# Two transformer blocks on one core: stage borders without drains, small products moved between slabs, and the state-space decays computed from one 128-row product

## What is computed

```python
def mla_branch(u, cos, sin, q_norm_g, w_uq, kv_norm_g, w_ukv, q_gain, k_gain):
    c_q, c_kv, k_rope = jnp.split(u, [MLA_Q_RANK, MLA_Q_RANK + MLA_KV_RANK], axis=-1)
    q = (rms_norm(c_q, q_norm_g) @ w_uq).reshape(Bsz, S, MLA_HEADS, MLA_QK_DIM)
    kv = (rms_norm(c_kv, kv_norm_g) @ w_ukv).reshape(Bsz, S, MLA_HEADS, MLA_NOPE + MLA_V)
...
def ssd_scan(x, dt, A, Bm, Cm):
    a_cum = jnp.cumsum(dtc * A.astype(jnp.float32).reshape(G, Hg), axis=2)
    seg = a_cum[:, :, :, None] - a_cum[:, :, None, :]
    decay = jnp.where(causal, jnp.exp(jnp.where(causal, seg, 0.0)), 0.0)
    cb = jnp.einsum('bcign,bcjgn->bcijg', Cc, Bc)
    y_diag = jnp.einsum('bcijg,bcijgh,bcjghp->bcighp', cb, decay, xdt)
...
def gated_linear_attention(q, k, v, r, a_lr, w_a2, b_a, norm_g):
    log_a = jax.nn.log_sigmoid(jnp.einsum('bsr,rk->bsk', a_lr.astype(f32), w_a2.astype(f32))
                               + b_a.astype(f32)) / GLA_TAU
```

## Time and profile before

| | us |
|---|---|
| median of 3 runs | 2051.41 (2048.81 to 2052.89) |
| profiled execution | 2049.72 |
| its span, first to last instruction | 2048.0 |
| TensorE busy | 2010.6 |
| VectorE busy | 1146.9 |
| ScalarE busy | 805.7 |
| GpSimd busy | 111.7 |

### The profile page before, as it was taken

How to read it: one execution, slowest core, us unless ns; L and a number is a source line. 1 busy time by engine, 2 the same in 40 slices (tenths; PEclk the granted TensorE clock), 3 DMA queues, 4 the chain that set the end, 5 groups by cost and what they waited for, 6 DMA issues and landing times.

```text
span 2048.0 us, 23834 instructions
## 1 busy us (share of the span) xinstructions
PE 2010.6 (98%) x9734; PEld 1649.8 (81%) x9734; DVE 1146.9 (56%) x1680; ACT 805.7 (39%) x1146; POOL 111.7 (5%) x120
## 2 busy tenths in 40 slices
PE   7999999999999999999999999999999999999998
PEld 6887788777888888888888687888888888888886
DVE  5757657577444666357468877743435444234346
ACT  5647543344422434134242634542323433123245
POOL 0004400221000000000010300000000000000000
PEclk9999999999999999999999999999999999999999
DMA  4320022212332333333332123223222232332222
GB/s 133 103 83 22 17 87 84 91 59 70 130 103 82 94 92 103 99 87 93 112 125 92 53 75 101 83 83 103 85 100 103 83 103 83 103 114 87 98 103 82
DMA packets 164443, 184.46 MB, mean 90 GB/s; under 512 B 6759, under 2 KB 125798, under 8 KB 164334
## 3 DMA queue, kind: packets, MB, share of 16 engines
q1 hardware_dynamic: 161006, 175.03, 26.8%
q10 hardware_dynamic: 2624, 5.78, 0.8%
q0 software_dynamic: 704, 2.13, 0.3%
HBM read 180.81 MB, written 2.12 MB: 89 GB/s over the span
## 4 chain that ended last, share of the span: by engine, by line
PE 94%; DVE 3%; issue 2%; ACT 1%; POOL 0%; DMA 0%; DVEq 0%; SPq 0%; POOLq 0%; ACTq 0%
PE ps L448 29%; PE ps L450 29%; PE ps L449 29%; PE ps L591 1%; PE ps L605 1%; PE ps L578 1%; PE ps L639 1%; DMA W<-in_w_in_dram 0%; PE ps L826 0%; ACT HH L1372 0%; DVE arena L2078 0%; PE ps L562 0%; DVE HL L1998 0%; DVE WL L1881 0%; PE ps L747 0%
## 5 line engine op out<-in xcount | busy, mean ns | idle before, releaser
L448 PE MATMUL ps<-HH,WH 128*128 128x512 f32 (+1 forms) x1464 | 561.6, 384 | 6.9 <-DVE HL L1998 2.9
L1881 DVE TENSOR_TENSOR WL<-W,WH 128x2048 fp32r<-128x2048 f32 (+2 forms) x162 | 366.5, 2263 | 355.7 <-ACT WH L1322 355.3
L450 PE MATMUL ps<-HH,WL 128*128 128x512 f32 (+1 forms) x1464 | 557.5, 381 | 0.0
L449 PE MATMUL ps<-HL,WH 128*128 128x512 f32 (+1 forms) x1464 | 557.4, 381 | 0.0
L1322 ACT ACTIVATE WH<-W 128x2048 fp32r<-128x2048 f32 (+2 forms) x163 | 307.2, 1886 | 290.3 <-DMA W<-in_w_ff_dram 116.2
L448 PEld LDWEIGHTS ps<-HH,WH 128*128 128x128 f32 x1464 | 276.2, 189 | 64.5 <-issue 6.6
L450 PEld LDWEIGHTS ps<-HH,WL 128*128 128x128 f32 x1464 | 275.9, 188 | 52.6
L449 PEld LDWEIGHTS ps<-HL,WH 128*128 128x128 f32 x1464 | 276.3, 189 | 51.8 <-issue 0.2
L448 PE MATMUL ps<-WH,arena_r 128*128 128x512 f32 (+1 forms) x616 | 239.6, 389 | 1.6 <-issue 1.6
L450 PE MATMUL ps<-WH,arena_r 128*128 128x512 f32 (+1 forms) x616 | 239.1, 388 | 0.0
L449 PE MATMUL ps<-WL,arena_r 128*128 128x512 f32 (+1 forms) x616 | 239.0, 388 | 0.0
(11 more groups left out here) (372 smaller groups left out, 2278.6 us busy)
## 6 DMA issues: line engine op xcount, KB each, us to landing
W<-in_w_in_dram SPq DMA_DIRECT2D x50, 1024.0 KB, 5.1
W<-in_w_ff_dram SPq DMA_DIRECT2D x32, 1024.0 KB, 5.2
W<-in_ffn_w_up_dram SPq DMA_DIRECT2D x44, 512.0 KB, 4.7
W<-in_w_gate_dram SPq DMA_DIRECT2D x16, 1024.0 KB, 5.0
W<-in_ffn_w_down_dram SPq DMA_DIRECT2D x10, 1024.0 KB, 5.0
W<-in_w_out_dram SPq DMA_DIRECT2D x8, 1024.0 KB, 5.1
W<-in_w_branch_dram SPq DMA_DIRECT2D x8, 1024.0 KB, 5.0
W<-in_w_br_ssm_dram SPq DMA_DIRECT2D x4, 1024.0 KB, 5.0
```

Of the source, the lines that this page charges most:

```text
L448: pe.matmul(out_, st[0], mv[0], start=first, stop=False)
L449: pe.matmul(out_, st[0], mv[1], start=False, stop=False)
L450: return pe.matmul(out_, st[1], mv[0], start=False, stop=last)
L1881: dve.tensor_tensor(WL[:, j % RING, 0:n], W[:, j % RING, 0:n], plain(WH[:, j % RING, 0:n]), ALU.subtract).then_inc(slab_lo, 1)
```

## The change

It does four things. (1) TensorE's drain at the end of each stage is gone; the other engines wait in `boundary` for a count of TensorE's results. (2) In mla the four parameter transposes stand between the two tiles of the second slab, and `kr` and `cstat` between the two halves of `uq`, with the splits of ScalarE and VectorE counted anew. (3) In the scan the row of sums is one product of 128 rows: its stationary operand U has ones in the rows 0 to 47 and the negated sums of the token tile in 64 to 111, and the moving one, written by GpSimd on all 128 rows, the diagonals and one-hot rows that pick the head. So PSUM holds a(i) - a(j) for four heads. ScalarE takes Relu of its negative into M, then Exp of the negative of that; `diff` is gone, and `mix` works in place in a ring of three. The diagonals have one buffer. The order of VectorE's and ScalarE's steps is changed, and the split of the next but one slab stands before the gates. (4) In gla the two `la` products stand behind the first token tile of `gv`.

```diff
--- before.py
+++ after.py
@@ -655,41 +660,44 @@
+                def parameters():
+                    pe.wait_ge(params_in, 16 * (len(place) - len(first_params)))
+                    for j in range(1, NPAR):
+                        b = bank(("par", j))
+                        pe.transpose(b[:, 0:P], rows[:, j, :], ident[:, :]).then_inc(pe_done, 1)
                 for i in range(2):
                     w = slab(KT, 256, win(256 * i, 256 * i + 256))
                     if i == 0:
                         gemm_f_by_halves("c", w, 2, first_parameters)
                     else:
-                        gemm_f("c", w, KT, 0, 2, hn, 2 * i)
+                        gemm_f("c", w, KT, 0, 2, hn, 2 * i, parameters)
                     slab_read()
-                    if i == 0:
-                        pe.wait_ge(params_in, 16 * (len(place) - len(first_params)))
-                        for j in range(1, NPAR):
-                            b = bank(("par", j))
-                            pe.transpose(b[:, 0:P], rows[:, j, :], ident[:, :]).then_inc(pe_done, 1)
...
-                taken(pe, ("c", 5))
-                b = bank("kr")
...
-                b = bank("cstat")
...
+                taken(pe, ("c", 2))
                 for half in range(2):
                     w = slab(3, 384, A["mla_w_uq"][0].rearrange("(k p) n -> p k n", p=P)[:, :, half * 384:half * 384 + 384])
                     gemm_t("uq", w, 3, 0, 384, lambda k, t: [c[:, k, t * P:(t + 1) * P] for c in cg], half)
                     slab_read()
+                    if half == 0:
+                        taken(pe, ("c", 5))
+                        b = bank("kr")
+                        for t in range(NT):
+                            tr = pe.transpose(b[:, t * ROPE:(t + 1) * ROPE], at(1024, S)[0:ROPE, t * P:(t + 1) * P],
+                                              ident[0:ROPE, 0:ROPE])
...
+                        b = bank("cstat")
+                        taken(pe, ("c", 4))
+                        pe.wait_ge(square_sums, 2)
...
@@ -793,11 +802,9 @@
                     def arow(q):
-                        i = 4 * t + q
-                        rs = slice(64 * (i % 2), 64 * (i % 2) + 48)
                         b = bank(("ai", t, q))
-                        pe.wait_ge(diagonals_ready, i + 1)
-                        pe.matmul(b[:, :], bc(unit[rs, 0:1], [48, P]), split_at(19456, S)[rs, :],
+                        pe.wait_ge(diagonals_ready, 4 * t + q + 1)
+                        pe.matmul(b[:, :], split_at(25088, NT, P)[:, t, :], split_at(19456, S),
                                   start=True, stop=True).then_inc(pe_done, 1)
@@ -823,7 +830,7 @@
                         pe.wait_ge(mix_ready, 4 * t + q + 1)
                         for j in range(4):
                             h = 4 * q + j
-                            mm = pe.matmul(b[:, (h % 8) * HD:(h % 8 + 1) * HD], M[:, q % 2, j, :],
+                            mm = pe.matmul(b[:, (h % 8) * HD:(h % 8 + 1) * HD], M[:, (4 * t + q) % 3, j, :],
                                            xdt[:, h * HD:(h + 1) * HD], start=True, stop=True)
+                def decays(t):
+                    if t == 0:
+                        pe.wait_ge(decay_in, 16)
+                        taken(pe, ("gasm", 0))
+                        for c in range(2):
+                            b = bank(("la", c))
+                            pe.matmul(b[:, :], wa2[0:16, c * P:(c + 1) * P], alr[0:16, :],
+                                      start=True, stop=True).then_inc(pe_done, 1)
+                gemm_t_long("gv", full, 1536, hnt, between=decays)
@@ -1131,7 +1141,7 @@
             for s in stages:
                 program[s]()
                 stage_slabs.append(len(slabs) - 1)
-                pe.drain().then_inc(tensor_end, 1)
+                stage_done.append(len(DONE))
         def boundary(eng, own, k):
 
             eng.drain().then_inc(own, 1)
-            for end in (tensor_end, scalar_end, vector_end, gpsimd_end):
+            eng.wait_ge(pe_done, stage_done[k])
+            for end in (scalar_end, vector_end, gpsimd_end):
                 if end is not own:
                     eng.wait_ge(end, k + 1)
                 def diagonal(i):
                     t, q = divmod(i, 4)
-                    rs = slice(64 * (i % 2), 64 * (i % 2) + 48)
-                    if i >= 2:
-                        use(pool, ("ai", (i - 2) // 4, (i - 2) % 4))
-                    pool.tensor_tensor(split_at(19456, 4, P)[rs], bc(plain(mask_r[rs, t * P:(t + 1) * P]).unsqueeze(1), [48, 4, P]),
-                                       bc(pick[rs, 4 * q:4 * q + 4].unsqueeze(2), [48, 4, P]), ALU.mult)\
+                    if i >= 1:
+                        use(pool, ("ai", (i - 1) // 4, (i - 1) % 4))
+                    pool.tensor_tensor(split_at(19456, 4, P), bc(plain(mask_r[:, t * P:(t + 1) * P]).unsqueeze(1), [P, 4, P]),
+                                       bc(pick[:, 4 * q:4 * q + 4].unsqueeze(2), [P, 4, P]), ALU.mult)\
...
                 diagonal(0)
-                diagonal(1)
...
+                    diagonal(4 * t + 1)
...
-                    for i in range(4 * t + 2, min(4 * t + 6, 4 * NT)):
+                    for i in range(4 * t + 2, min(4 * t + 5, 4 * NT)):
                         diagonal(i)
...
-                split(slab_of["kr"] + 2)
+                split(slab_of["c", 5] + 2)
-                tmp, xt = at(24576, 2, 512), at(12288, NT, DM)
+                M, xt = at(23552, 3, 512), at(12288, NT, DM)
 
                 def decay(i):
+                    b = use(act, ("ai", i // 4, i % 4))
+                    if i >= 3:
+                        t, q = divmod(i - 3, 4)
+                        use(act, ("yd", t, q // 2)) if q % 2 == 1 else act.wait_ge(yc_ready, 2 * t + q // 2 + 1)
+                    freed(act.activation(M[:, i % 3, :], b[:, :], ACT.Relu, scale=-1.0), ("ai", i // 4, i % 4))
                     taken(act, ("ai", i // 4, i % 4))
-                    act.activation(tmp[:, i % 2, :], tmp[:, i % 2, :], ACT.Exp).then_inc(decay_ready, 1)
+                    act.activation(M[:, i % 3, :], M[:, i % 3, :], ACT.Exp, scale=-1.0).then_inc(decay_ready, 1)
                 for t in range(NT):
+                    decay(4 * t)
+                    decay(4 * t + 1)
                     if t > 0:
                         sum_squares(t - 1)
-                    decay(4 * t)
-                    if t > 0:
                         scale(t - 1)
-                    decay(4 * t + 1)
+                    split(scan_slab(2 * t) + 2)
                     for n, kind, cc, j in SCAN_GATES[2 * t]:
                         gate_out("G1", n, kind, cc, j)
                     decay(4 * t + 2)
                     decay(4 * t + 3)
+                    split(scan_slab(2 * t + 1) + 2)
                     for n, kind, cc, j in SCAN_GATES[2 * t + 1]:
                         gate_out("G1", n, kind, cc, j)
+                split(slab_of["gv", 0, 0])
...
-                split(slab_of["gv", 0, 0])
...
-                split(slab_of["kr"] + 1)
+                split(slab_of["c", 5] + 1)
...
+                split(slab_of["c", 5] + 2)
                 b = use(dve, "kr")
...
-                split(slab_of["kr"] + 2)
-                dve.tensor_copy(unit[:, :], ones[:, 0:1])
+                dve.memset(plain(mask_r[:, :]), 1.0)
+                link(dve.memset(pick[:, :], 0.0))
...
-                dve.tensor_copy(mask_r[64:112, :], plain(mask_r[0:48, :]))
...
-                M, tmp = at(23552, 2, 4, P), at(24576, 2, 512)
+                M, U = at(23552, 3, 4, P), split_at(25088, S)
+                link(dve.memset(plain(U), 1.0))
+                dve.tensor_scalar(U[64:112, :], plain(mask_r[0:48, :]), -1.0, None, ALU.mult).then_inc(sums_turned, 1)
...
-                    if t > 0:
-                        variance(t - 1)
-
-                    def diff(q):
-                        i = 4 * t + q
-                        b = use(dve, ("ai", t, q))
-                        for j in range(4):
-
-                            sl = slice(j * P, (j + 1) * P)
-                            ins = dve.tensor_scalar(tmp[:, i % 2, sl], b[:, sl], TS[:, t, 4 * q + j:4 * q + j + 1],
-                                                    0.0, ALU.subtract, ALU.min)
-                        freed(ins, ("ai", t, q))
 
                     def mix(q):
                         i = 4 * t + q
                         taken(dve, ("cb", t))
                         dve.wait_ge(decay_ready, i + 1)
-                        if q >= 2:
-                            dve.wait_ge(yc_ready, 2 * t + 1) if q == 2 else use(dve, ("yd", t, 0))
-                        dve.tensor_tensor(M[:, q % 2], tmp[:, i % 2, :].rearrange("p (h i) -> p h i", h=4),
-                                          bc(cbm[:, q // 2:q // 2 + 1, :], [P, 4, P]), ALU.mult)\
-                            .then_inc(mix_ready, 1)
-                        dve.wait_ge(mix_ready, i + 1)
-
```

(27 more changed lines are left out.)

36 lines of the change are left out of this document (14 added, 22 removed).

## The result

The changed kernel takes 2024.43 us (2023.48 to 2025.37, 4 runs) against 2052.15 for the kernel before in the same comparison (2048.81 to 2053.01, 4 runs): 27.7 us less. The two profiled executions differ by less, 2049.72 to 2025.37, 24.35 us. The prediction was 2027.3 with 2020 to 2037, and 24.1 us for the profiled execution.

The account below looks back on a forecast made before the run. TensorE, busy 98% of the span, was taken as the bound, so only gaps between passes could be won. 7.2 + 4.1 + 1.65 - 0.3 + 5.35 + 4.4 + 2.5 = 24.9, less 0.8, gave 2027.3 us, range 2020 to 2037.

Parts of the forecast that it names:

- Part 1: Stage borders: removing TensorE's drains wins 0.50 or 0.42 us at fourteen, 0.6 at five before norms; 7.2 us, bounds 5.5 and 9.
- Part 2: Parameter transposes in mla: moving them removes 2.4 us idle and a 1.7 us low-clock loss; 4.1 us, bounds 2.4 and 4.2.
- Part 3: kr and cstat in mla: 0.8 us idle plus 0.85, half a low-clock loss; 1.65 us, less 0.3 for the move's cost.
- Part 4: Row of sums in the scan: 128-row products cost about an ordinary pass; 5.35 us over 16, bounds nothing and 16 x 0.40.
- Part 5: Scan waits: low-part waits and low clock go, 1.4 us of bank wait stays; 4.4 us won, bounds 2 and 5.8.
- The third rival: Scan: ScalarE becomes the new wait through Relu, table load and Exp; 9 us come back, 2036 us, chance 0.08.
- Part 6: The la products in gla: idle, late neighbours and low clock before and behind them go; 2.5 us, bounds 1 and 2.8.
- The sum: Whole kernel: the terms add to 24.9 us, 24.1 after a deduction, giving 2025.6 us profiled and 2027.3 median.
- the 0.8 that I took off: Whole kernel: deduction of 0.8 us for waits that come late next, such as a bank or a first pass.
- the row: Scan's row of sums: array rows don't matter, so 5.35 us of gain are missing; 2032.7 us, chance 0.12.
- The low clock: Four half-clock stretches in mla, scan and la stay or move elsewhere; 5.95 us missing, 2033 us, chance 0.15.
- The single buffer of diagonals: Scan: one buffer chains POOL, TensorE and ScalarE, making TensorE wait up to 16 times; slower, 2059 us at 2 each, chance 0.04.

Follow-up runs that it names:

- the run of this part alone: Kernel before with only TensorE's drains at the 20 stage borders replaced by waits for a count of results: median 2042.41 us, ratio 0.9961.
- second profile: Profile of the unchanged changed kernel, run once more beside the kernel before: 2025.18 us against 2048.39, ratio 0.9886.

## Why the prediction was right, by its steps

**Part 1, 7.2 us.** Measured 7.2 as a sum and by the run of this part alone. Two terms were off and cancelled, which is luck. Behind small fp32 products a border was worth 0.50 like any other (14 x 0.50 = 7.0, not 6.6). The surcharge of 0.08 on the pass after stayed there, as forecast; it is the first pass that came earlier by 0.50 and not by 0.42 (it stood 0.53 behind the last small product at 522.35 and stands 0.02 behind it at 506.44). And the borders ahead of a norm gave 0.2, not 0.6, since VectorE's chain ends at the same time.

**Part 2, 4.1 us.** Measured 4.3: +4.8 where the waits were, -0.5 for the transposes at their new place.

**Part 3, 1.65 - 0.3.** 2.3 in the first profile, 0.7 in the second. I had counted half of the low stretch, since the one-column products stay (they are eight, recorded as sixteen, and not fifteen as I wrote). Of the nine profiled kernels with this move in the form of the change, five had the stretch near 59 us and four had not. Over these nine the term is 1.4 on average, close to my 1.35, but as a mean of two outcomes and not as half a stretch. The waits that I feared for a bank or a slab of `uq` never came.

**Part 4, 5.35 us.** About 6.0: 16 x 0.38. The reading that the cost of L800 lay in the 48-row form was right and is now shown, and the broadcast column, which I had named beside it, cost nothing. The load of 182 ns against 188 ns told nothing on this: the load is as long, but with 48 rows it doesn't lie beside the pass before, and the load behind it doesn't lie beside the 48-row product either. The rule of the Trainium skill (TensorE: Matmul & The Clock Gate, section LDWEIGHTS (loading the stationary operand)) agrees with these two numbers and would have given 5.35 too little, because it speaks of the length of a load and not of what it overlaps.

**Part 5, 4.4 us.** 3.9: 9.9 in the scan less 6.0. The waits for low parts and their low clock went; the wait for the bank of `yd` stayed and grew from 1.0 to 1.36 with its surcharge, as the 1.4 left for it had it, and at L2344 0.5 stands where 0.2 stood. The mechanism was told too loosely, though: I named the clamps that leave VectorE and the early splits in one breath, as if either would do. The run without the early splits shows that the other changes by themselves bring three waits of 9.1 us in all, where two of 2.7 in all stood in the kernel before, so the early splits are what the gain hangs on; how much the clamps add to them stays open. The third rival had named ScalarE as the new wait, and in that run it is.

**Part 6, 2.5 us.** 2.0 in the changed kernel, 2.4 alone. The difference is a wait of 0.3 and its surcharge 0.1 for the low part of the first `gv` slab. In the kernel with la alone that part is ready at 1235.83 and TensorE begins the slab at 1236.12; in the changed kernel it is ready at 1216.64, and TensorE, which is there earlier, begins at 1216.70. It is the one place where two parts of the change met.

**The sum.** 25.7 us by places, against 24.9 in the sum; the 0.8 that I took off for waits that come late next had no row, and in its place the runs show the 0.4 at la and 0.3 more at L2344, and the places hold these already. The start of the profiled execution cost 1.6 (passes at 0.21 us instead of 0.12 up to 17.4 us, and a first pass 0.7 later). It varies from execution to execution: in the second profile of the same kernel it cost nothing. With the 0.3 that has no place, the passes gained 24.4 in all, and the profiles differ by 24.35. That the forecast of 24.1 comes so close is in part luck: the places gave more and the start took it back. The forecast time of 2027.3 is 2.9 over the measured 2024.43, since I took the sum off a median of 2051.41 that was high: in the later comparisons the kernel before took 2048.39 to 2049.63. The rivals: the row didn't keep its price. The low clock stayed in part, behind cstat, in about half of the executions. ScalarE didn't wait, thanks to the splits. The single buffer of diagonals never showed: TensorE has no wait for GpSimd in the scan.

## What to carry to other kernels

On an engine that is busy 98% of the span, cost an edit by the starts of consecutive instructions and not by durations or idle time, and set two kernels against each other by the n-th instruction of a kind that both have; that gives the price of an edit of 0.4 us in one execution, where medians of the same kernel before differed by 3.8 us between two comparisons. Before an engine's steps are put in another order, look for the step that waits for the middle of the next piece of work, and move what others need ahead of it. Small products are worth placing between two tiles of a large product, where the 0.8 us for a copy or the 2.4 us for a bank were covered here, and among full passes a product in the 128-row form costs one pass, where the 48-row one cost nearly three (0.63 against 0.227 us).

## What the runs showed of the hardware

A 48-row product between 128-row ones cost 0.6 us in all, its weight load of 182 ns starting with the product and not with the pass before, a 128-row one with the same columns 0.23; a stationary operand that is one column broadcast costs no more than a full tile. The 3.4 us at half clock behind a wait are not repeatable: the same wait of 0.8 us at the la products was followed by 3.4 us, by 6.8 us and by none in three kernels that are alike there. In the feed-forward net sixteen waits that cost 0.5 to 2.2 us had none behind them and four that cost 3.0 to 3.6 had one each. A 512-column VectorE product in SBUF took 0.69 us alone and 0.8 to 2.4 when it began beside a GpSimd instruction, and it ended 0.55 us behind that instruction in nine cases of nine in the changed kernel.
